# Strassen slices of a two-layer decoder step: weight factors split a unit earlier, VectorE's adds ahead of its splits, the next square moved

## What is computed

```python
D_MODEL = 1024
D_FF = 4 * D_MODEL
def rms_norm(x, g):
    y = xf * lax.rsqrt(jnp.mean(xf * xf, axis=-1, keepdims=True) + EPS)
    return (y * g.astype(jnp.float32)).astype(x.dtype)
def sqrelu_mlp(h, w_up, w_down):
    return jnp.square(jax.nn.relu(h @ w_up)) @ w_down
def reference(...):
    for i in range(DEPTH):
        hp = rms_norm(xp, norm_mix[i])
        ...
        xp = xp + op
        xp = xp + sqrelu_mlp(rms_norm(xp, norm_mlp[i]), mlp_w_up[i], mlp_w_down[i])
        ...
```

## Times and profile before

| | us |
|---|---|
| median of 3 runs | 2373.12 |
| lowest and highest | 2371.97, 2374.85 |
| the profiled execution | 2373.27 |
| its span | 2371.5 |

### The profile page before, as it was taken

How to read it: one execution, slowest core, us unless ns; L and a number is a source line. 1 busy time by engine, 2 the same in 40 slices (tenths; PEclk the granted TensorE clock), 3 DMA queues, 4 the chain that set the end, 5 groups by cost and what they waited for, 6 DMA issues and landing times.

```text
span 2371.5 us, 40596 instructions
## 1 busy us (share of the span) xinstructions
PE 2309.7 (97%) x15837; PEld 2243.5 (95%) x15837; DVE 1329.1 (56%) x2152; ACT 784.9 (33%) x1600; POOL 482.4 (20%) x467
## 2 busy tenths in 40 slices
PE   8999999999999999999999999999999999999999
PEld 8997899999999999999999998889999999999999
DVE  6449724657667566565623326545656655656653
ACT  6549722323322323323300016423232332332312
POOL 1005400322323323210000004001232332322300
PEclk9999999999999999999999999999999999999999
DMA  8622030111111111121411126421111111111112
GB/s 228 85 45 78 11 101 20 44 54 45 35 53 47 37 49 44 44 80 36 130 38 36 58 87 182 142 99 36 54 36 53 36 44 53 37 51 53 35 62 74
DMA packets 180407, 150.48 MB, mean 63 GB/s; under 512 B 34525, under 2 KB 170041, under 8 KB 180140
## 3 DMA queue, kind: packets, MB, share of 16 engines
q1 hardware_dynamic: 177356, 136.18, 19.9%
q0 software_dynamic: 2720, 12.56, 1.7%
q10 hardware_dynamic: 224, 0.23, 0.0%
HBM read 126.50 MB, written 24.47 MB: 64 GB/s over the span
## 4 chain that ended last, share of the span: by engine, by line
PE 86%; DVE 6%; ACT 3%; issue 3%; POOL 2%; DMA 0%; DVEq 0%; ACTq 0%; POOLq 0%
PE ps L1972 16%; PE ps L1973 16%; PE ps L1976 16%; PE ps L339 8%; PE ps L343 8%; PE ps L340 8%; PE ps L355 3%; PE ps L362 1%; DVE act_sq L1769 1%; DVE f_lo L1714 1%; PE ps L590 1%; DVE ring_lo L1661 1%; PE ps L1072 1%; PE ps L1048 1%; POOL act_sq L1737 1%
## 5 line engine op out<-in xcount | busy, mean ns | idle before, releaser
L1972 PE MATMUL ps<-f_hi,ring_hi 128*128 128x268 f32 (+1 forms) x1568 | 424.0, 290 | 44.9 <-DVE x L1784 38.5
L1973 PE MATMUL ps<-h_lo,ring_hi 128*128 128x352 f32 (+2 forms) x1440 | 466.8, 325 | 0.0
L1972 PE MATMUL ps<-h_hi,ring_hi 128*128 128x352 f32 (+2 forms) x1440 | 466.6, 325 | 0.0
L1973 PE MATMUL ps<-f_lo,ring_hi 128*128 128x268 f32 (+1 forms) x1568 | 421.9, 289 | 0.0
L1784 DVE TENSOR_TENSOR x<-x,ps 128x536 f32<-128x536 f32 (+1 forms) x392 | 277.4, 708 | 174.5 <-PE ps L1976 172.9
L1972 PEld LDWEIGHTS ps<-f_hi,ring_hi 128*128 128x128 f32 x1568 | 300.9, 192 | 47.8 <-issue 41.0
L1976 PE MATMUL ps<-f_hi,ring_lo 128*128 128x268 f32 (+1 forms) x1568 | 323.4, 288 | 0.0
L1976 PE MATMUL ps<-h_hi,ring_lo 128*128 128x352 f32 (+2 forms) x1440 | 313.2, 325 | 0.0
L1973 PEld LDWEIGHTS ps<-f_lo,ring_hi 128*128 128x128 f32 x1568 | 300.6, 192 | 0.0
L1972 PEld LDWEIGHTS ps<-h_hi,ring_hi 128*128 128x128 f32 x1440 | 271.4, 188 | 0.0
L1973 PEld LDWEIGHTS ps<-h_lo,ring_hi 128*128 128x128 f32 x1440 | 271.1, 188 | 0.0
(11 more groups left out here) (374 smaller groups left out, 3614.1 us busy)
## 6 DMA issues: line engine op xcount, KB each, us to landing
ring_raw<-in_mlp_w_up SPq DMA_DIRECT2D x60, 512.0 KB, 4.0
ring_raw<-in_mlp_w_down SPq DMA_DIRECT2D x56, 512.0 KB, 3.4
raw<-in_mlstm_w_in SPq DMA_DIRECT2D x12, 1024.0 KB, 5.3
x<-scratch_x SPq DMA_DIRECT2D x8, 537.0 KB, 6.2
scratch_x<-x POOLq DMA_DIRECT2D x1, 4296.0 KB, 12.1
x<-scratch_x SPq DMA_DIRECT2D x8, 528.0 KB, 4.8
x_tok<-in_x_prompt SPq DMA_DIRECT2D x8, 512.0 KB, 7.6
raw<-in_attn_w_qkv SPq DMA_DIRECT2D x16, 256.0 KB, 7.5
```

The costliest lines, as they stand in the source:

```text
L1972: nc.tensor.matmul(o, wh, hi[:, c], start=start, stop=False, skip_group_check=chained)
L1973: nc.tensor.matmul(o, wh, lo[:, c], start=False, stop=False, skip_group_check=chained)
```

## The change

In `mlp_slice_pool` the sums n = 1 and n = 2 of pair 0 join n = 0, ahead of the activation sums 1 to 3 of half 1. In `mlp_slice_act` and `mlp_slice_dve` the splits of weight factors m = 0, 1 and 2 move ahead of the square and the relu of block 3, to the unit before; m = 3, 4 and 5 take the places among the activation factors, and m = 6 stands behind them. ACT squares block 4 after splitting m = 12, no longer ahead of m = 7. In DVE's loop over the products the add of m stands ahead of the split of m + 7; the split of the next up weights stands behind the add of m = 21, as before. PE and SP have the same instructions in the same order.

```diff
@@ mlp_slice_pool
-            weight_sum_pool(pool, layer, i, 0, 0)
+            for n in range(3):
+                weight_sum_pool(pool, layer, i, 0, n)
             for n in range(1, 4):
                 t_pool(pool, layer, i, 1, n)
             for p in range(PAIRS):
-                for n in range(1, 4):
+                for n in range(1 if p else 3, 4):
                     weight_sum_pool(pool, layer, i, p, n)
@@ mlp_slice_act
+            prod_hi(act, layer, i, 0)
             factor_hi(act, layer, i, 1, 1, entry)
+            prod_hi(act, layer, i, 1)
+            prod_hi(act, layer, i, 2)
 
             square_act(act, layer, i, 3)
-            for f, m in ((3, None), (2, None), (4, 0), (5, 1), (6, 2)):
+            for f, m in ((3, None), (2, 3), (4, 4), (5, None), (6, 5)):
                 factor_hi(act, layer, i, 1, f, entry)
                 if m is not None:
                     prod_hi(act, layer, i, m)
-            for m in range(3, 7):
-                prod_hi(act, layer, i, m)
-
-            square_act(act, layer, i, 4)
+            prod_hi(act, layer, i, 6)
+
             for m in range(7, NPROD):
                 prod_hi(act, layer, i, m)
+                if m == 12:
+                    square_act(act, layer, i, 4)
@@ mlp_slice_dve
+            prod_lo(dve, layer, i, 0)
             factor_lo(dve, layer, i, 1, 1)
+            prod_lo(dve, layer, i, 1)
+            prod_lo(dve, layer, i, 2)
 
             relu_dve(dve, layer, i, 3, i * NFAC + 7)
-            for f, m in ((3, None), (2, None), (4, 0), (5, 1), (6, 2)):
+            for f, m in ((3, None), (2, 3), (4, 4), (5, None), (6, 5)):
                 factor_lo(dve, layer, i, 1, f)
                 if m is not None:
                     prod_lo(dve, layer, i, m)
-            for m in range(3, 7):
-                prod_lo(dve, layer, i, m)
+            prod_lo(dve, layer, i, 6)
 
             relu_dve(dve, layer, i, 4, i * NFAC + NFAC)
             for m in range(NPROD):
+                add_dve(dve, layer, i, m, x)
                 if m + 7 < NPROD:
                     prod_lo(dve, layer, i, m + 7)
-                if m == 22:
+                if m == 21:
                     ring_unit_lo(dve, layer, 1, ring_hi_ready, since("ring_hi_ready", layer, i * EVENTS + (E_J1 + 1)), ring_lo_ready)
-                add_dve(dve, layer, i, m, x)
```

## The result

The changed kernel takes 2312.57 us (median of 4 runs, 2311.75 to 2313.91); the kernel before took 2373.98 beside it (2371.97 to 2377.1). The ratio is 0.9738, with a 95% interval of 0.9726 to 0.975. The forecast was 2313, from 2309 to 2330.

A forecast was written before the change was run, and what follows sets the result against it. TensorE was taken to bound the kernel, busy 2309.7 of 2371.5 us, so only idle time or slowed work could be won. Excesses 24.2 + 36.3 = 60.5; 2373.1 - 60.5 = 2312.6, rounded 2313, range 2309 to 2330.

The forecast's parts named there:

- What bounds it: TensorE's wait at the first matmul of a product, once in each of 14 Strassen slices, at most 3.2 us, 44.9 together.
- the 14 stretches: Seven in each layer, each from product 0 of a slice to the next up unit, 27 products long.
- What the wait costs: Excess of the stretches from product 0 to the next up unit: 24.2 us in layer 0, 36.3 in layer 1.
- The clock: In layer 1 TensorE's clock falls behind the wait, mostly 1.2 GHz for 2.4; 12.1 of the 36.3 us.
- Splits of m = 0, 1, 2 early: On ACT and DVE, done near 532.3, relu of block 3 starts at 534.07; cover 1.7 us, so cost nothing.
- DVE between the relus: Between relus of blocks 3 and 4 seven splits become four; DVE free between 544.8 and 546.3, taken as 545.8.
- The spare: The relu of block 4 may start 0.67 us late before TensorE waits at product 2; residual wait taken as 0.
- What is late next: In the products, P3, later P6, the moved square and the next slice's first raw load: each costs nothing.
- The relu beside a POOL sum: If a POOL sum held up the relu of block 4, about 0.1 us a slice, 1.4 in all; by the rule 0.

## Why the prediction was right

- *What bounds it*: TensorE's one wait in 14 places. Right: with it gone, nothing else moved (60.0 of 60.2 us lie in the 14 stretches).
- *What the wait costs*, read as the length of the stretch and not as the idle time. Right, and it mattered: the idle time alone, 44.9 us, would have given 2328. 27 products take 39.96 and 39.46 us where 39.99 and 39.37 were worked out; 24.2 + 36.3 were forecast, 24.4 + 35.6 came.
- *The clock* comes back with the wait. Right in its size: 12.1 was forecast, and 35.6 - 24.4 = 11.2 measured if the wait costs as much in layer 1 as in layer 0. Against the one stretch of layer 1 with the wait and without a fall it is 311.87 - 7 x 42.84 = 12.0. The sentence that nothing but the wait precedes a fall holds, and what makes a wait a harmful one was not known then and isn't now.
- *Splits of m = 0, 1, 2 early*, done near 532.3 of the old clock, 1.7 us ahead of relu 3. In the changed kernel the last ends at 528.86 and relu 3 starts at 530.49, 1.6 later.
- *DVE between the relus*: free 0.14 after product 0 by the forecast (545.8 against 545.66), 0.14 measured. The agreement to the hundredth is luck: 545.8 was chosen between 544.8 and 546.3, and the row given for it, factor 6 with "two splits to go", has five splits behind it in the earlier trace rows; two is the changed order. POOL's two sums did stand beside factors 4 and 5 and the split of m = 4, as laid out.
- *The spare*: 0.67 forecast as the delay that PE doesn't feel. By the start of product 2 it is about 0.75; the 0.63 and 0.66 of the stretches have the slow restart in them.
- *What is late next*: nothing. The stretches have no loss at the places of P3.
- *The relu beside a POOL sum*, and the rule of the Trainium skill ("SBUF — State Buffer", "Who interferes with whom") by which it costs nothing: the trace of after has no such overlap either, since the sums end at 540.4 and the relu starts at 542.28. For the relu it stays untested here. The add, which also has one input in SBUF and one in PSUM, was beside POOL's sums in both kernels. In after, in the second slice of layer 0, nearly the whole of this add lies beside two of them:

```profile
549.67 0.71 DVE L1785 TENSOR_TENSOR x<-x,ps 128x536 f32<-128x536 f32 x1 [0.43 <-PE ps L1982]
549.32 0.74 POOL L1683 TENSOR_TENSOR ring_raw<-ring_raw 128x256 f32<-128x256 f32 x1 [1.40 <-DVE ring_lo L1661]
550.01 0.74 POOL L1673 TENSOR_TENSOR ring_raw<-ring_raw 128x256 f32<-128x256 f32 x1
```

  Of the adds of after, the 84 that have POOL's sums beside more than half of them take 0.70 to 0.72, and the 308 with none beside them take 0.69 to 0.72. The factors, with both inputs in SBUF, take 1.24 to 1.87 with sums beside them and 0.69 to 0.72 without. For the add and the factors the trace agrees with that rule.
- Where it was loose: the three edits were costed as if each did its share. The prediction never said that the square's move and the order of add and split are alternatives, and that either could have been left out.

## What to carry to other kernels

A wait that ends with one engine's instruction is the end of a chain through several queues; follow it back to the first link that is late without need, and cost each edit by the link that it takes out. Edits that remove the same link don't add up, and one that shortens the chain behind a later link brings only the difference. Price a recurring wait by the length of the stretch around it against the same work without a wait, not by the idle time that the view of waits gives: here that was 60 us for 45.

## What the runs showed of the hardware

- Waits of TensorE of one length, 3.2 us, are followed by a stretch at half the clock or not, in one and the same kernel, and nine matmuls fewer in a slice turned it on for a whole layer: in the profiled executions the work fell by 11.8 us and the falls gave 10.4 back. In the nine kernels whose products waited by 1.7 us or less none was followed by one.
- A DVE instruction that stands in the queue with nothing to wait for costs some 0.07 us apart from its columns: from their start to that of the next instruction 256 columns took 0.33 us as one instruction, 1.37 as 16 and 2.47 as 32.
- A DVE instruction with one input in SBUF and one in PSUM was not held up by POOL's sums, one with both inputs in SBUF was: 0.72 at most for the add, up to 1.87 for a factor that takes 0.70 alone.
